# A two-layer decoder step on one core: pieces of the second output group placed one step earlier around the last two local groups

## The chip, the cores and the metric

The kernel runs on one core of a Trainium2 chip. The metric is device time in microseconds (us) of one execution. The kernel before was timed in three runs: 1675.39, 1678.78 and 1682.44 us, the median is 1678.78.

## What is computed

The reference is one inference step of a small hybrid decoder with two layers, D_MODEL 1024, over a prompt of 2048 tokens and a sample group of 8 x 8 tokens. Both layers have the same frame: an RMSNorm, one input projection, a token mixer and a cross-attention into 256 memory tokens, each multiplied by the SiLU of its gate, and one output projection that is added to the residual. The first layer's mixer pools over windows of rows. The second layer's mixer is local attention: 12 query heads on 4 shared key/value heads, blocks of 128 tokens that see their own and the previous block, with a learned sink in the softmax.

```python
z = rms_norm(x, norm_b[j]) @ w_in_b[j]
q, gq, qm, gm = jnp.split(z, [SWA_W, 2 * SWA_W, 2 * SWA_W + MEM_W], axis=-1)
q = rope_partial(rms_norm(q.reshape(B, T, N_Q_HEADS, HEAD_DIM), q_norm[j]), pos)
...
    o = swa_banded(q, k, v, sinks[j])
...
ys = o * jax.nn.silu(gq)
ym = memory_branch(qm, gm, mem_q_norm[li], mem_k[li], mem_v[li])
x = x + jnp.concatenate([ys, ym], axis=-1) @ w_out_b[j]
```

## The kernel before

All engines run a program written out by hand, and semaphores tie them together. The prompt is cut into 8 tiles of 256 tokens. The first layer goes over its 8 tiles and the sample group, then the second layer ("B") over the same 8 tiles and the sample group ("SB"). The loop of the second layer (`for it in range(TILES // 2): for p in range(2)`) has the same order of work for each tile on every engine.

Projections are exact to more than half precision: weights and activations are split into a high and a low f16 part, and three matmuls (high x high, high x low, low x high) stand for each product, accumulated in PSUM (`PARTS`). The gated activations that go into the output projection are eight chunks of 128 features, chunks 0 to 5 from the local attention and 6 and 7 from the memory branch. `split_out(part, t, g, kcs, halves, first, whole)` (matmul at line 791) issues the matmuls of output group g (256 features, two halves of 128) for the chunks in kcs, three for each chunk and half. So `split_out("B", t, 1, (0, 1), halves=(0,))` is six matmuls. With `first=True` and half 0 it first waits until the bank of PSUM is free:

```python
b = Z.wait_free(pe, part, t, f"out{g}") if first and 0 in halves else Z.bank(part, f"out{g}")
```

The banks of `ps_z` are a ring of two (class `Ring`): the names of a tile take them in turn, and a name waits until the reader of the name two places ahead has released it. The order of a tile of the second layer is

```python
"B": ["kv0", "kv1", "qa0", "qb0", "qa1", "qb1", "gm", "g0", "g1", "g2", *OUT],
```

with `OUT` being out0 to out3. g0 to g2 are the gates of the local attention; VectorE's `silu` (line 1714) reads them from `ps_z` and releases their banks.

Local attention works on six groups a tile, `W6 = [(0, 0), (1, 0), (0, 1), (1, 1), (0, 2), (1, 2)]` (block of 128 tokens, four heads). A group goes through these steps:

- `window_scores` on TensorE, then `window_front` on VectorE (masks and the maximum) and `window_exps` on ScalarE (line 1483)
- `window_back` on VectorE (the sum, its reciprocal, line 2158), then `window_norm` on GpSimd (line 2482)
- `window_transposes` on TensorE (line 1058, waits for `pw_norm`), then `window_weights` on VectorE (line 2166, two masked copies out of `ps_t`)
- `window_values` on TensorE (line 1070, waits until `ps_t` has been read), then `window_gated` on VectorE (line 2175, multiplies with the gate)

When both groups of a pair of chunks are gated, ScalarE takes the high half (`gate_highs`, line 1265), VectorE the low half as a subtraction (`gate_lows`, line 1740), and `glow_in` lets TensorE use these chunks. VectorE's order at the end of the tile is

```python
window_gated(t, 3)
window_weights(t, 4)
silu("B", t, "g2", 9, 4)
window_back(t, 5)
window_gated(t, 4)
gate_lows("B", t, 2, 2)
window_weights(t, 5)
window_gated(t, 5)
gate_lows("B", t, 3, 4)
```

In the same stretch ScalarE squares the next tile's input (`squares_x`, line 1222, after the high half of chunks 2 and 3), and GpSimd adds up the squares in three sums (`sums`, lines 2318, 2320, 2322). Their result is read by TensorE in `square_sums` (line 644) after the output groups 0 and 1 are whole. From there come the next tile's normalised input and its first projections.

Of the kernel before, what the change touches and what calls it, by code (L numbers as in the profile page):

```python
# [170 lines left out]
def build(nc, io):  # L171
    with ExitStack() as ctx:
# [461 lines left out]
        def _(pe):  # L634
# [150 lines left out]
            def split_out(part, t, g, kcs, halves=(0, 1), first=False, whole=False):  # L785

                b = Z.wait_free(pe, part, t, f"out{g}") if first and 0 in halves else Z.bank(part, f"out{g}")
                for half in halves:
                    for kc in kcs:
                        for ws, x in PARTS:  # L790
                            last = mm(ps_z[:, b, half * NT:(half + 1) * NT],  # L791
                                      w_out_split[:, g, ws, kc, half * P:(half + 1) * P], gate_parts[x][:, kc, 0:NT],
                                      start=(first and half == 0 and kc == kcs[0] and ws + x == 0),
                                      stop=(whole and half == 1 and kc == kcs[-1] and ws == 1))
                if whole:
                    last.then_inc(Z.full[b], 1)
# [257 lines left out]
            def window_transposes(t, i):  # L1054
                pe.wait_ge(pw_norm.sem, pw_norm.after("B", t, i))
                T.wait_free(pe, "B", t, f"ptw{i}")
                for e in range(4):
                    last = tr(ps_t[:, e * P:(e + 1) * P], sw[:, i % 2, e, :], ident)  # L1058
                last.then_inc(T.full[0], 1)

            def window_values(t, p, i):
                blk, gi = W6[i]
                T.wait_read(pe, "B", t, f"ptw{i}")
                V.wait_free(pe, "B", t, f"pvw{i}")
                own = 2 * p + blk
                for c in range(2):
                    for j, (s, w) in enumerate((((own - 1) % 4, ptp), (own, ptc))):
                        for par in range(2):
                            kv = 2 * ((2 * gi + c) // 3) + par
                            last = mm(ps_p[par * HD:(par + 1) * HD, c * P:(c + 1) * P],  # L1070
                                      v[:, s, kv * HD:(kv + 1) * HD], w[:, par * 2 + c, :],
                                      start=(j == 0), stop=(j == 1), skip_group_check=True)
                last.then_inc(V.full[0], 1)

            for it in range(TILES // 2):
                for p in range(2):
                    t = it * 2 + p
# [61 lines left out]
                    split_out("B", t, 0, (0, 1, 6, 7), halves=(0,), first=True)  # L1139
                    window_transposes(t, 4)  # L1140
                    split_out("B", t, 0, (0, 1, 6, 7), halves=(1,), first=True)
                    window_values(t, p, 4)
                    split_out("B", t, 1, (0, 1), halves=(0,), first=True)
                    window_transposes(t, 5)
                    split_out("B", t, 1, (6, 7), halves=(0,))
                    split_out("B", t, 1, (0, 1), halves=(1,), first=True)
                    window_values(t, p, 5)
                    split_out("B", t, 1, (6, 7), halves=(1,))
                    pe.wait_ge(glow_in.sem, glow_in.after("B", t, 2))
                    split_out("B", t, 0, (2, 3))  # L1150
                    split_out("B", t, 1, (2, 3))
# [1499 lines left out]
```

## Time and profile before

| | |
|---|---|
| median of three runs | 1678.78 us (1675.39 to 1682.44) |
| the profiled execution, its own time | 1681.61 us |
| its span, first to last instruction | 1679.5 us |
| TensorE matmul busy | 1560.9 us, 93% |
| VectorE busy | 956.4 us, 57% |
| ScalarE busy | 511.9 us, 30% |
| GpSimd busy | 506.6 us, 30% |
| mean granted clock of TensorE | 0.971 |
| HBM traffic | 71 GB/s over the span |

Busy shares are averages over stages of different kinds. Matmuls are pipelined and their ends are modelled, so the start of one to the start of the next is a better measure than the duration of one (0.27 us each, 0.11 us from start to start). In the order of time a row has the start in us from the beginning of the span, the duration, engine, line, operation, output <- inputs and count; an idle time of the engine ahead of it stands in brackets with what ended it. PE is TensorE, DVE is VectorE, ACT is ScalarE, POOL is GpSimd.

### The profile page before, as it was taken

To read this page: it belongs to the slowest core of one execution; us is meant where nothing else is said; L and a number is where in the kernel's file an instruction comes from. 1 tells how busy PE (TensorE), PEld (TensorE's weight loads), DVE (VectorE), ACT (ScalarE), POOL (GpSimd) and SP (SyncE) were. 2 spreads that over 40 slices of the span, in tenths; PEclk is the share of its full clock that TensorE was granted. 3 is DMA by queue.
4 is the path that set the end of the run, shared out by engine and by line. 5 is a ranking of instruction groups with operands and counts; after the bars stand their busy time and mean duration, and the time that the engine had idled before them with its cause. 6 is when DMAs were issued, how large, how long until landed. Compare 5 with 4: busy or idle time off the path is not lost.

```text
span 1679.5 us, 31237 instructions
## 1 busy us (share of the span) xinstructions
PE 1560.9 (93%) x13448; PEld 1223.0 (73%) x13448; DVE 956.4 (57%) x1846; ACT 511.9 (30%) x1227; POOL 506.6 (30%) x377
## 2 busy tenths in 40 slices
PE   4787999999999999978999999999999999999966
PEld 2466888888888888864775767768586685767745
DVE  6876465556646464624663836647375573846632
ACT  2442232232313232311432414224142331414320
POOL 3641425242425233221423313132131322224210
PEclk9999999999999999987999999999999999999985
DMA  9120213122121213178001010100101001010140
GB/s 399 48 82 29 98 60 117 66 86 101 51 101 51 102 62 114 55 279 348 1 7 45 2 51 2 39 13 2 51 2 51 1 2 51 2 51 2 41 148 26
DMA packets 27400, 119.12 MB, mean 71 GB/s; under 512 B 3488, under 2 KB 3936, under 8 KB 16480
## 3 DMA queue, kind: packets, MB, share of 16 engines
q1 hardware_dynamic: 25184, 108.33, 17.3%
q10 hardware_dynamic: 2080, 8.80, 1.3%
q8 instruction: 107, 1.75, 0.4%
q14 instruction: 29, 0.24, 0.0%
HBM read 81.38 MB, written 37.64 MB: 71 GB/s over the span
## 4 chain that ended last, share of the span: by engine, by line
PE 77%; DVE 13%; POOL 4%; ACT 2%; DMA 2%; issue 2%; SPq 0%; DVEq 0%; POOLq 0%; ACTq 0%
PE ps_z L677 23%; PE ps_z L791 18%; PE ps_z L666 16%; PE ps_z L781 3%; PE ps_s L1050 2%; PE ps_z L849 2%; PE ps_p L760 2%; DVE ph_sb L2166 2%; PE ps_t L750 2%; POOL tiny_sb L2313 2%; PE ps_p L1070 1%; PE ps_s L742 1%; POOL pm_sb L2337 1%; PE ps_t L1058 1%; DMA w_x_sb<-mem_vs 1%
## 5 line engine op out<-in xcount | busy, mean ns | idle before, releaser
L677 PE MATMUL ps_z<-xn_sb,w_in_sb 128*128 128x256 f16 (+1 forms) x4752 | 502.4, 264 | 5.1 <-DVE gate_sb L1714 4.2
L677 PEld LDWEIGHTS ps_z<-xn_sb,w_in_sb 128*128 128x128 f16 x4752 | 426.2, 98 | 62.4 <-issue 8.8
L791 PE MATMUL ps_z<-pm_sb,w_out_sb 128*128 128x256 f16 x2048 | 352.3, 274 | 3.3 <-DVE x_buf_sb L1780 3.3
L791 PE MATMUL ps_z<-gate_sb,w_out_sb 128*128 128x256 f16 x1024 | 280.3, 274 | 0.0
L2313 POOL TENSOR_TENSOR tiny_sb<-tiny_sb 128x2 f32<-128x2 f32 (+4 forms) x56 | 94.2, 1682 | 537.7 <-DVE tiny_sb L1681 305.5
L791 PEld LDWEIGHTS ps_z<-pm_sb,w_out_sb 128*128 128x128 f16 x2048 | 202.5, 99 | 32.2 <-issue 4.8
L666 PE MATMUL ps_z<-w_in_sb,xn_sb 128*128 128x512 f16 (+2 forms) x840 | 181.7, 376 | 0.0
L1672 DVE TENSOR_REDUCE tiny_sb<-scr_sb 128x8 f32<-128x512 f32 (+3 forms) x64 | 38.0, 593 | 237.3 <-ACT scr_sb L1230 157.4
L666 PEld LDWEIGHTS ps_z<-w_in_sb,xn_sb 128*128 128x128 f16 (+1 forms) x840 | 82.9, 99 | 94.1 <-issue 0.2
L1230 ACT ACTIVATE scr_sb<-ps_z,tiny_sb 128x256 f32<-128x256 f32 (+2 forms) x94 | 42.6, 489 | 347.1 <-PE ps_z L666 271.2
L2482 POOL TENSOR_TENSOR ph_sb<-ph_sb,tiny_sb 128x512 f32<-128x512 f32 x48 | 52.9, 1102 | 192.6 <-DVE tiny_sb L2158 192.6
L791 PEld LDWEIGHTS ps_z<-gate_sb,w_out_sb 128*128 128x128 f16 x1024 | 100.6, 98 | 11.6
L1483 ACT ACTIVATE ph_sb<-ph_sb,tiny_sb 128x128 f32<-128x128 f32 x192 | 74.5, 390 | 91.9 <-DVE tiny_sb L2148 91.9
L1780 DVE SCALAR_TENSOR_TENSOR x_buf_sb<-ps_z,tiny_sb,x_buf_sb 128x512 f32<-128x512 f32 x64 | 48.0, 750 | 91.5 <-PE ps_z L791 91.4
L2415 POOL TENSOR_TENSOR ph_sb<-ph_sb 128x1080 f32<-128x1080 f32 (+6 forms) x56 | 75.0, 1340 | 70.5 <-ACT ph_sb L1361 67.9
L666 PE MATMUL ps_z<-w_x_sb,xn_sb 128*128 128x512 f16 (+1 forms) x408 | 92.3, 387 | 3.4 <-issue 3.4
L2348 POOL TENSOR_TENSOR pm_sb<-pm_sb,tiny_sb 128x1024 f32<-128x1024 f32 x32 | 62.3, 1958 | 77.9 <-DVE tiny_sb L1707 77.9
L2318 POOL TENSOR_TENSOR big_sb<-big_sb 128x1024 f32<-128x1024 f32 x17 | 40.0, 2354 | 144.5 <-ACT big_sb L1222 144.5
L1244 ACT ACTIVATE xn_sb<-big_sb 128x2048 f16<-128x2048 f32 x18 | 34.4, 1910 | 149.5 <-DVE big_sb L1603 149.5
L666 PEld LDWEIGHTS ps_z<-w_x_sb,xn_sb 128*128 128x128 f16 (+1 forms) x408 | 40.8, 100 | 51.7 <-issue 7.3
L1275 ACT ACTIVATE scr_sb<-ps_z,tiny_sb 128x512 f32<-128x512 f32 (+1 forms) x72 | 46.7, 649 | 87.1 <-PE ps_z L677 85.4
L1280 ACT ACTIVATE big_sb<-ps_t 128x512 f32<-128x512 f32 (+1 forms) x68 | 39.5, 581 | 98.2 <-PE ps_t L750 82.0
(275 smaller groups left out, 2384.6 us busy)
## 6 DMA issues: line engine op xcount, KB each, us to landing
x_buf_sb<-x SPq DMA_DIRECT2D x18, 1024.0 KB, 4.8
w_x_sb<-w_b SPq DMA_DIRECT2D x14, 1024.0 KB, 4.8
x<-x_buf_sb SPq DMA_DIRECT2D x9, 1024.0 KB, 3.9
y<-x_buf_sb SPq DMA_DIRECT2D x9, 1024.0 KB, 3.9
w_in_sb<-w_in_a SPq DMA_DIRECT2D x8, 1024.0 KB, 25.5
w_in_sb<-parts ACTq DMA_DIRECT2D x8, 1024.0 KB, 13.2
parts<-ph_sb SPq DMA_DIRECT2D x14, 512.0 KB, 3.0
parts<-w_x_sb SPq DMA_DIRECT2D x14, 512.0 KB, 3.0
```

The costliest lines, as they stand in the source:

```text
L666: last = mm(out, xs[:, x, kc, tok:tok + n], w[:, gs[0]:gs[-1] + 1, ws, kc, :], start=(kc == 0 and ws + x == 0), stop=(kc == KC - 1 and ws ...
L677: last = mm(ps_z[:, b, half * NT:half * NT + n], w_split[:, g, ws, kc, half * P:(half + 1) * P], xs[:, x, kc, 0:n], start=(kc == 0 and ws ...
L781: last = mm(out, mix_w[:, blocks.index((o, i)), :], src, start=(i == ins[0]), stop=(i == ins[-1]))
L791: last = mm(ps_z[:, b, half * NT:(half + 1) * NT], w_out_split[:, g, ws, kc, half * P:(half + 1) * P], gate_parts[x][:, kc, 0:NT], start=( ...
L1230: last = f(scr[0:n, b, i * w:(i + 1) * w], ps_z[0:n, b, i * w:(i + 1) * w], ACT.Square, scale=unit if isinstance(unit, float) else unit[0:n])
L1275: f(pair[0], pair[1], ACT.Tanh, scale=halfunit).then_inc(scr_in.sem, 1)
L1483: f(sw[:, n % 2, e, :], sw[:, n % 2, e, :], ACT.Exp, bias=w_neg[:, n % 2, e:e + 1], scale=SCALE, accum_out=w_sum[:, n % 2, e:e + 1])
L1780: ve.scalar_tensor_tensor(x, ps_z[:, b].rearrange("p (c n) -> p c n", c=2)[:, :, 0:n], unit, x, ALU.mult, ALU.add).then_inc(Z.free[b], 1)
L2313: return tt(out, x, power[0:n, 0:w], ALU.pow)
L2348: tt(pm[:, blk], pm[:, blk], r, ALU.mult).then_inc(pm_norm.sem, 1)
L2415: own(tt(out[..., at:UW], src[..., at:UW], src[..., at // 2:UW - at // 2], ALU.add))
L2482: tt(sw[:, i], sw[:, i], r, ALU.mult).then_inc(pw_norm.sem, 1)
```

## The change

On TensorE alone, in the loop of the second layer, three pieces of output group 1 of six matmuls each stand one place earlier: chunks (0, 1) of half 0 ahead of the values of group 4, chunks (6, 7) of half 0 ahead of the transposes of group 5, chunks (6, 7) of half 1 ahead of the values of group 5. The order among the pieces of `split_out` stays as it was.

```diff
                     split_out("B", t, 0, (0, 1, 6, 7), halves=(0,), first=True)
                     window_transposes(t, 4)
                     split_out("B", t, 0, (0, 1, 6, 7), halves=(1,), first=True)
+                    split_out("B", t, 1, (0, 1), halves=(0,), first=True)
                     window_values(t, p, 4)
-                    split_out("B", t, 1, (0, 1), halves=(0,), first=True)
+                    split_out("B", t, 1, (6, 7), halves=(0,))
                     window_transposes(t, 5)
-                    split_out("B", t, 1, (6, 7), halves=(0,))
                     split_out("B", t, 1, (0, 1), halves=(1,), first=True)
+                    split_out("B", t, 1, (6, 7), halves=(1,))
                     window_values(t, p, 5)
-                    split_out("B", t, 1, (6, 7), halves=(1,))
                     pe.wait_ge(glow_in.sem, glow_in.after("B", t, 2))
                     split_out("B", t, 0, (2, 3))
                     split_out("B", t, 1, (2, 3))
```

## Rows read from the trace of the kernel before

**Rows 1.** The page: the chain that ended last, shares of the span by engine.
```profile
PE 77%; DVE 13%; POOL 4%; ACT 2%; DMA 2%; issue 2%; SPq 0%; DVEq 0%; POOLq 0%; ACTq 0%
```

**Rows 2.** TensorE's waits, whole span: us in total, times, longest us.
```profile
PE ps_p L1070 <- DVE ph_sb L2166: 12.0, 16, 1.3
```

**Rows 3.** The last chain in order of time: start us, us, what.
```profile
862.30 6.00 PE ps_z L791 x54
...
1576.52 6.00 PE ps_z L791 x54
```

**Rows 4.** Order of time, TensorE, 953 to 971 us (one tile's output stretch).
```profile
957.63 0.27 PE L791 MATMUL ps_z<-pm_sb,w_out_sb 128*128 128x256 f16 x1
959.19 1.09 PE L1070 MATMUL ps_p<-ph_sb 128*64 128x128 f32 x16 [1.29 <-DVE ph_sb L2166]
...
961.19 0.66 PE L1058 MATMUL ps_t<-small_sb,ph_sb 128*128 128x128 f32 x4
...
963.23 1.09 PE L1070 MATMUL ps_p<-ph_sb 128*64 128x128 f32 x16
964.26 0.28 PE L791 MATMUL ps_z<-pm_sb,w_out_sb 128*128 128x256 f16 x1
...
970.16 0.50 PE L644 MATMUL ps_p<-ones_sb,big_sb 128*128 128x1 f32 x4
```

**Rows 5.** Order of time, VectorE, the same stretch.
```profile
957.86 1.28 DVE L2166 TENSOR_TENSOR ph_sb<-ps_t,small_sb 128x512 f32<-128x512 f32 x2
959.05 0.68 DVE L1714 SCALAR_TENSOR_TENSOR gate_sb<-scr_sb,ps_z 128x512 f32<-128x512 f32 x1
...
960.33 0.48 DVE L2175 SCALAR_TENSOR_TENSOR gate_sb<-ps_p,tiny_sb,gate_sb 128x256 f32<-128x256 f32 x1 [0.32 <-PE ps_p L1070]
960.74 0.95 DVE L1740 TENSOR_TENSOR gate_sb<-gate_sb,pm_sb 128x512 f16<-128x512 f32 x1
961.89 1.29 DVE L2166 TENSOR_TENSOR ph_sb<-ps_t,small_sb 128x512 f32<-128x512 f32 x2 [0.20 <-PE ps_t L1058]
...
965.55 1.23 DVE L1740 TENSOR_TENSOR gate_sb<-gate_sb,pm_sb 128x512 f16<-128x512 f32 x1 [0.70 <-ACT pm_sb L1265]
```

**Rows 6.** Order of time, GpSimd, the same stretch.
```profile
960.10 1.04 POOL L2482 TENSOR_TENSOR ph_sb<-ph_sb,tiny_sb 128x512 f32<-128x512 f32 x1 [4.76 <-DVE tiny_sb L2158]
961.73 2.36 POOL L2318 TENSOR_TENSOR big_sb<-big_sb 128x1024 f32<-128x1024 f32 x1 [0.59 <-ACT big_sb L1222]
964.17 1.27 POOL L2320 TENSOR_TENSOR big_sb<-big_sb 128x512 f32<-128x512 f32 x1
965.52 0.73 POOL L2322 TENSOR_TENSOR big_sb<-big_sb 128x256 f32<-128x256 f32 x1
```

**Rows 7.** Order of time, ScalarE, the same stretch.
```profile
959.76 1.90 ACT L1222 ACTIVATE big_sb<-x_buf_sb 128x2048 f32<-128x2048 f32 x1
964.89 0.63 ACT L1265 ACTIVATE pm_sb<-gate_sb 128x512 f16<-128x512 f32 x1 [3.24 <-DVE gate_sb L2175]
```

**Rows 8.** Instructions of two VectorE lines: duration ns min/median/max, first and last start us.
```profile
L1740 DVE TENSOR_TENSOR gate_sb<-gate_sb,pm_sb x64: 658/692/1246, 144.5 to 1577.7; 128x512 f16<-128x512 f32 x64
...
L2156 DVE TENSOR_TENSOR tiny_sb<-tiny_sb x48: 150/159/860, 823.0 to 1571.8; 128x4 f32<-128x4 f32 x48
```

**Rows 9.** Order of time, GpSimd and VectorE, about 937 and 152 us.
```profile
935.82 1.89 POOL L2348 TENSOR_TENSOR pm_sb<-pm_sb,tiny_sb 128x1024 f32<-128x1024 f32 x1 [2.73 <-DVE tiny_sb L1707]
936.87 0.86 DVE L2156 TENSOR_TENSOR tiny_sb<-tiny_sb 128x4 f32<-128x4 f32 x1 [0.62 <-ACT tiny_sb L1485]
...
150.54 2.35 POOL L2318 TENSOR_TENSOR big_sb<-big_sb 128x1024 f32<-128x1024 f32 x1 [25.69 <-ACT big_sb L1222]
151.62 1.35 DVE L1623 TENSOR_SCALAR lo_sb<-small_sb,tiny_sb 128x128 f32<-128x128 f32 x1
152.96 1.27 POOL L2320 TENSOR_TENSOR big_sb<-big_sb 128x512 f32<-128x512 f32 x1
```

**Rows 10.** One stretch: us, engines' busy us (x instructions), PEclk, DMA share, GB/s.
```profile
953.60:970.20 16.60, 15.06 (x154) 12.68 (x154) 11.32 (x23) 5.23 (x13) 6.79 (x5) 1.00 0.00 1
```

## The prediction

> **What bounds the kernel now.** I read the page first [rows 1]: the chain that ended last is 77% TensorE, so a change in the order of its work counts only through the gaps that it closes or opens. The list of waits says where such gaps are [rows 2]: the values of the local groups (line 1070) waited for VectorE's masked weights (line 2166) 16 times, 12.0 us in all, which is two waits in each of the eight tiles of the second layer. The eight tiles repeat each other: the chain in order of time has an entry for line 791 in each, 54 matmuls in 6.00 us, the first at 862.30 and the last at 1576.52, seven periods of 102.03 [rows 3]. The remaining views are orders of time in the second tile, where this entry comes at 964.3.
>
> In it I follow TensorE [rows 4]. The last piece of group 0, half 1, starts at 957.63, and matmuls of this kind follow each other at 0.109 us (964.26 to 970.16 for 54), so TensorE is free at 957.74. The values of group 4 start only at 959.19. That is gap 1, 1.45 us. The six matmuls of out1 (0,1) follow, then the transposes of group 5 at 961.19, 0.31 us after the last of the six could have ended (gap 2), and the values of group 5 at 963.23, 0.24 us after the twelve matmuls between (gap 3). So 2.0 us a tile, 16 us in the kernel, is the most that any order here could win.
>
> **Who ends each gap.** VectorE's rows [rows 5]: the masked weights of group 4 run from 957.86 to 959.14, and the values start 0.05 later. Gap 2 ends with GpSimd's normalisation of group 5 (960.10 for 1.04) [rows 6], gap 3 with the masked weights of group 5, 961.89 to 963.18. The reader should also see what stands between them on VectorE: the SiLU of g2 (line 1714, 959.05 for 0.68), the gating of group 4 (line 2175, 960.33), the low half of gate chunks 2 and 3 (line 1740, 960.74), and only then the weights of group 5.
>
> **The change, step by step.** No instruction is added or taken away, none is a DMA, and no other engine's order is edited. Three groups of six matmuls move.
>
> Step 1, out1 (0,1) half 0 goes ahead of the values of group 4. It carries first=True for half 0, so it waits for its bank of ps_z to come free. The order of the Z ring has g2 at place 9 and out1 at place 11 of the tile, and two banks: the same one. g2 is released by the SiLU at line 1714, and on VectorE that stands behind the masked weights of group 4, for which the values wait. So the piece that was to fill gap 1 can't start before 959.73 + 0.05 = 959.78 [rows 5], later than the values started before. The six matmuls take 0.65, and the values of group 4, queued behind them, start at 960.43 instead of 959.19: **1.24 us later**. Gap 1 grows from 1.45 to 2.04.
>
> Step 2, out1 (6,7) half 0 goes ahead of the transposes of group 5. The values of a group issue for 1.03 (963.23 to 964.26), those of group 4 now to 961.46; six matmuls bring it to 962.12; by then the normalisation of group 5 has been done since 961.14, so gap 2 is gone. The transposes start at 962.12 against 961.19, and VectorE could read them 0.70 later, as before (961.19 to 961.89), at 962.82.
>
> Step 3, out1 (6,7) half 1 goes ahead of the values of group 5. TensorE has twelve matmuls after the transposes (1.31 after about 0.45) and reaches the values at about 963.9. It then depends on when VectorE has the weights of group 5.
>
> Step 4 is what the delay of step 1 does on VectorE. The gating of group 4 waits for the values: their last matmul ends 1.09 after their start, at 961.52, and the gating starts 0.05 later, 961.57; the low half of chunks 2 and 3 follows 0.41 later as in the rows, at **961.98** instead of 960.74. GpSimd starts its first sum of squares, 128x1024, at **961.73** and holds on to 964.09 [rows 6]. That start does not move: it follows ScalarE's squares, 959.76 for 1.90 [rows 7], which wait for nothing that is changed. Now the low half is a subtraction of two SBUF tensors, and such operations stand still while GpSimd runs one of its own on SBUF tensors [rows 8, 9]: line 1740 takes 0.658 at best, and in this tile 0.95 and 1.23, where it met a GpSimd instruction; both ended 0.55 and 0.53 after that instruction's end (961.14 to 961.69, 966.25 to 966.78). A four-element addition (line 2156) that takes 0.159 in the median took 0.86, from 936.87 to 937.73, against a GpSimd instruction that ended at 937.71. And the very instruction at issue, line 2318, did it at 150.54 to 152.89: a scaling of one 128x128 SBUF tensor (line 1623) started at 151.62 and ended at 152.97, just after the release. So the low half will hold VectorE until 964.09 + 0.54 = 964.63. In order behind it, the masked weights of group 5 start at about 964.57 and end at 965.86 (1.29), and the values of group 5 start at **965.91** instead of 963.23. Gap 3 grows from 0.24 to 2.0.
>
> On this the Trainium skill speaks against the change too ("SBUF — State Buffer", where it treats the shared port pair): VectorE operations with two SBUF inputs and GpSimd operations that read SBUF take one lock, whoever starts first keeps it for the whole instruction, and the other blocks fully. The rows agree as to the blocking; by the letter of the rule the whole 0.66 of the subtraction would come after the release, 0.12 a tile more than the 0.54 that the rows show, and the sum would be 17 us instead of 16.
>
> **The sum.** The values of group 5 issue for 1.03, to 966.94. Six of the 54 matmuls that followed them now lie ahead, so 48 remain, 5.25 us, and the sums of the square (line 644), the next step, start at 972.19 instead of 970.16: **+2.03 us a tile, +16.2 for eight**. Two covers must hold. The chain to gate chunk 4 (gating 0.48, ScalarE's high half 0.63 [rows 7], low half) runs from the values' last result at 967.00 to about 968.9; TensorE wants it after 24 of the 48 matmuls, at 969.56, so it stays hidden by 0.6. GpSimd's remaining sums are put back by the subtraction by about half a microsecond, to 966.8, and are wanted at 972. All that follows in the tile is released by what has moved with it, so I take nothing off later.
>
> The profiled execution took 1681.61 us; with the sum 1697.8. It lies 2.8 above the median of the runs shown, 1678.78, which with the sum gives **1695.0**.
>
> **Rivals.**
> A. As above, 1695.0. The uncertain term is the stand-still of the low half. From below it is nothing (its 0.66 then lies ahead of the transposes' result); from above it loses the port a second time (D). I take the stand-still for all of line 2318, because the rows show just that instruction doing it [rows 9].
>
> B, on the other side: not slower. The low half gets the port first, or is not held. It decides at one point, whether 961.98 lies before or after GpSimd's 961.73, a margin of 0.25 that I worked out and did not see. Then the weights of group 5 follow the transposes, 962.82 to 964.11, the values start at 964.16, and the tile is 0.28 longer: +2.2 us, **1681**. For it: the margin is only a quarter of a microsecond. Against it: the end of the SiLU's row would have to be 0.25 early as a release, while the release that ended gap 1 came 0.05 after its row's end; and the port went to GpSimd on a lead of only 0.03 at 965.52 against 965.55.
>
> C. The bank does not bind, and the change does what its order suggests. Then the six matmuls run in gap 1, the values of both groups start when they did, and six matmuls fewer follow them: 0.65 a tile, 5.2 in all, **1673.6**, 0.3% faster. Against it stand the order of the ring and the place of the SiLU.
>
> D. VectorE loses the port again, to the second sum of GpSimd (964.17 to 965.44). The low half then ends at 965.98, and the tile is 3.4 longer: **1706**. Against it: at 152.89 the waiting VectorE operation got through before the second sum, at 152.96, had run [rows 9].
>
> E. TensorE's clock. With two gaps of 2.0 us inside eight microseconds it could fall. In the stretch of 953.6 to 970.2, with gap 1 at 1.45, the granted clock is 1.00, that is 2.4 GHz throughout [rows 10]. At 1.2 GHz the 48 matmuls would take another 5.25, for eight tiles 42 us, **1737**. The Trainium skill ("TensorE: Matmul & The Clock Gate", Part 1) has an idle array fall back to 1.2 GHz; no row here shows that at gaps of 2 us.
>
> **How the numbers follow.** Chances: A 0.81, B 0.10, C 0.04, D 0.03, E 0.02. About 0.5%, 8.4 us, is what a measurement of this kernel can tell from no change. A, D and E lie beyond it on the slow side: 0.85, after taking a little off for the size of A. B and C lie within it: 0.13. Faster by more would need over half of all three gaps, and no case gives that: 0.02. A's own range is 1690 to 1700: 3 or 4 us of scatter between runs, as those shown have (1675.39 to 1682.44), and a microsecond for the rule above. A alone is just 8 in 10, and scatter takes some of it, so the range goes down to B: 1680 to 1700.
>
> **What would show it.** Right: the first piece of out1 waits for line 1714 (gap of about 2.0); the values of group 4 start 1.2 us later in the tile; line 1740 has one instance in each tile of about 2.6 us that ends half a microsecond after line 2318; the values of group 5 wait about 2.0 for line 2166; the period is 104.05. Wrong: a line 1740 of 0.7 with line 2318 starting after it is B; a first piece at 957.74 is C; a line 1740 of 4 us is D; a granted clock below 1 in the tile is E.

## The result, and the profile after

The changed kernel takes 1695.8 us (median of four runs, 1694.7 to 1697.12), the kernel before beside it 1679.74 (1675.39 to 1682.44). The ratio is 1.0094, with a 95% interval of 1.0078 to 1.0110: slower, by 16 us. The profiled execution took 1697.12 us, its span is 1695.1.

The waits of TensorE over the whole span (us in total, times, longest) hold a new one at the top, and the old one of [rows 2] has not gone:

```profile
PE ps_z L791 <- DVE gate_sb L1714: 15.1, 8, 1.9
PE ps_p L1070 <- DVE ph_sb L2166: 13.9, 15, 1.7
```

The first is step 1 of the prediction: in each of the eight tiles the first matmul of out1 waits for the SiLU of g2, which releases its bank. The second counts other waits than it did. Before, its 16 were those of the values of group 3 (0.22 each) and of group 4 (gap 1, 1.29 each) in the eight tiles. Now the eight of group 3 remain, and the other seven are gap 3, about 1.74 each; the second tile has none, since its matmuls ahead of gap 3 were slow (see the section on the prediction). Gap 1 no longer shows as a wait for the masked weights, since they are done 1.4 us before TensorE gets there.

The chain in order of time gives the period. It shows the 48 matmuls that are left behind the values of group 5, where [rows 3] had 54:

```profile
864.67 5.35 PE ps_z L791 x48
...
1592.89 5.35 PE ps_z L791 x48
```

Seven periods lie between the two, so one is 104.03 us, against 102.03 before: 2.00 us a tile, 16.0 in eight. The whole change of time lies in this stretch of the tile.

To lay a tile of after over the one of before, I take the values of group 3 as its zero; the work that leads to them is not touched. Before, in the tile that the prediction follows, they start here:

```profile
953.63 1.09 PE L1070 MATMUL ps_p<-ph_sb 128*64 128x128 f32 x16 [0.22 <-DVE ph_sb L2166]
```

I take the third tile of after, because the second has a stretch at a lower clock. There TensorE does this (order of time, values, transposes and the first matmul of out1):

```profile
1059.35 1.09 PE L1070 MATMUL ps_p<-ph_sb 128*64 128x128 f32 x16 [0.21 <-DVE ph_sb L2166]
...
1065.51 0.28 PE L791 MATMUL ps_z<-pm_sb,w_out_sb 128*128 128x256 f16 x1 [1.89 <-DVE gate_sb L1714]
...
1066.27 1.09 PE L1070 MATMUL ps_p<-ph_sb 128*64 128x128 f32 x16
...
1067.96 0.60 PE L1058 MATMUL ps_t<-small_sb,ph_sb 128*128 128x128 f32 x4
...
1071.61 1.09 PE L1070 MATMUL ps_p<-ph_sb 128*64 128x128 f32 x16 [1.74 <-DVE ph_sb L2166]
...
1077.89 0.51 PE L644 MATMUL ps_p<-ones_sb,big_sb 128*128 128x1 f32 x4
```

VectorE and GpSimd in the same tile:

```profile
1064.78 0.68 DVE L1714 SCALAR_TENSOR_TENSOR gate_sb<-scr_sb,ps_z 128x512 f32<-128x512 f32 x1
...
1067.41 0.48 DVE L2175 SCALAR_TENSOR_TENSOR gate_sb<-ps_p,tiny_sb,gate_sb 128x256 f32<-128x256 f32 x1 [1.67 <-PE ps_p L1070]
1067.82 2.54 DVE L1740 TENSOR_TENSOR gate_sb<-gate_sb,pm_sb 128x512 f16<-128x512 f32 x1
1070.28 1.27 DVE L2166 TENSOR_TENSOR ph_sb<-ps_t,small_sb 128x512 f32<-128x512 f32 x2
```
```profile
1067.45 2.36 POOL L2318 TENSOR_TENSOR big_sb<-big_sb 128x1024 f32<-128x1024 f32 x1 [0.59 <-ACT big_sb L1222]
1069.89 1.60 POOL L2320 TENSOR_TENSOR big_sb<-big_sb 128x512 f32<-128x512 f32 x1
```

The reader sees the whole mechanism in these lines. The SiLU ends at 1065.46, and the first matmul of out1 starts 0.05 later. The values of group 4 follow, late; with them the gating (line 2175) is late, and the low half (line 1740) starts at 1067.82, 0.37 behind GpSimd's first sum. It takes 2.54 us for a subtraction that takes 0.66 alone, and ends at 1070.36, 0.55 after the sum's end. Seven tiles are like this one. In the second the low half starts later, 0.60 behind the sum, and takes 2.30; its end is again 0.56 after the sum's end. Behind it the masked weights (line 2166) are late, and TensorE waits 1.74 us for them. Even the second sum bears the trace of it: 1.60 against 1.27 in [rows 6], and it starts 0.47 before the low half ends.

### The profile page after: what moved, and what is told of

It reads as the page before. It is cut to its first block, busy times and chain, and to the rows that moved or that the text cites. A ratio compares the mean times of both kernels' runs of the same rounds, so it can differ in the third digit from the quotient of the medians.

```text
span 1695.1 us, 31237 instructions
## 1 busy us (share of the span) xinstructions
PE 1560.6 (92%) x13448; PEld 1223.7 (72%) x13448; DVE 963.8 (57%) x1846; ACT 511.9 (30%) x1227; POOL 509.1 (30%) x377
## 4 chain that ended last, share of the span: by engine, by line
PE 77%; DVE 14%; POOL 3%; ACT 2%; DMA 2%; issue 2%; SPq 0%; DVEq 0%; POOLq 0%; ACTq 0%
PE ps_z L677 23%; PE ps_z L791 18%; PE ps_z L666 16%; PE ps_z L781 3%; PE ps_s L1050 2%; PE ps_z L849 2%; PE ps_p L1070 2%; PE ps_p L760 2%; PE ps_t L750 2%; DVE ph_sb L2166 2%; POOL tiny_sb L2313 2%; DVE gate_sb L1740 1%; PE ps_s L742 1%; POOL pm_sb L2337 1%; DMA w_x_sb<-mem_vs 1%
## 5 line engine op out<-in xcount | busy, mean ns | idle before, releaser
L1265 ACT ACTIVATE pm_sb<-gate_sb 128x512 f16<-128x512 f32 x64 | 40.1, 626 | 114.2 <-DVE gate_sb L2175 47.2
```

## The experiments

Times in the tile are given from the start of the values of group 3. They are alike in all tiles of each trace, to 0.02, but for tiles with a lower clock: the six under the mark *, and the first tile of the kernel whose sums wait (told at the end of the section on the prediction). The columns are the start of the values of group 4, of the values of group 5, and of the sums of the square (line 644), where the next step begins. The table was worked out from the order of time of each trace. The ratios are estimated from all executions and can differ in the fourth place from the quotient of the medians.

```
kernel                          group 4   group 5   line 644   ratio to before (95%)
before                            5.56      9.60     16.53     1
after                             6.92     12.25     18.53     1.0094 (1.0078 to 1.0110)
sums wait for the low half        6.91     10.59     16.87     1.0012 (1.0004 to 1.0021)
wait for the bank alone           6.15      9.83     16.76     1.0012 (1.0003 to 1.0021)
first move alone                  6.91     12.25     20.8 *    1.0184 (1.0170 to 1.0198)
second and third move alone       5.56      9.89     16.17     0.9976 (0.9966 to 0.9985)
SiLU first                        6.16      9.83     16.11     0.9984 (0.9975 to 0.9993)
gap filled                        6.37      9.60     15.87     0.9966 (0.9953 to 0.9979)
* 20.6 to 20.8 in six tiles, 19.18 in two
```

**The sums wait for the low half.** The changed kernel with one wait more, on GpSimd:

```diff
+                    pool.wait_ge(glow_in.sem, glow_in.after("B", t, 2))
                     sums("B", t, 0)
```

> The changed kernel, and GpSimd's sums of squares (lines 2318 to 2322) wait for the low half of gate chunks 2 and 3, so that these two can't meet; the wait of out1 for its bank stays. Theory: of the 2.0 us a tile, most is the low half standing still (2.54 in the changed kernel against 0.66). Without it the values of group 4 still start 6.92 after those of group 3 (5.56 before), the masked weights of group 5 follow the transposes, and the values of group 5 start at about 10.65 after those of group 3 instead of 12.25 (9.60 before); the tile is about 0.4 longer than before: 1680 + 3 = 1683 us. Rival: the wait for the bank (or TensorE's clock behind the longer gaps) is the loss by itself; then the time stays near 1696.

Measured: 1684.41 us against 1681.79 for the kernel before on that chip. Taking away the meeting of the two instructions gives back 1.66 of the 2.00 us a tile (18.53 to 16.87). The added wait also starts the sums 1.1 us later in the tile; line 644 still does not wait for them. In the second tile of this kernel, VectorE's low half and GpSimd's sum, which starts behind it:

```profile
963.74 0.68 DVE L1740 TENSOR_TENSOR gate_sb<-gate_sb,pm_sb 128x512 f16<-128x512 f32 x1
```
```profile
964.50 2.36 POOL L2318 TENSOR_TENSOR big_sb<-big_sb 128x1024 f32<-128x1024 f32 x1 [1.72 <-DVE gate_sb L1740]
```

The rival, that the wait for the bank is the loss by itself, has fallen: the wait is still there (15.0 us in all, eight times), and the tile is 0.34 longer than before, with what the other two moves win already in it.

**The wait for the bank alone.** The kernel before, with the wait put ahead of the values of group 4 and the matmuls left behind them:

```diff
+                    Z.wait_free(pe, "B", t, "out1")
                     window_values(t, p, 4)
                     split_out("B", t, 1, (0, 1), halves=(0,), first=True)
```

> The kernel before, with only the wait for out1's bank put ahead of the values of group 4; the matmuls stay where they were. The values of group 4 are late by about 0.6 instead of 1.36, and the low half of chunks 2 and 3 starts about 0.4 ahead of GpSimd's first sum, so it takes the port first. Theory (the loss has a threshold, the point at which the low half comes behind the sum's start): low half of 0.7 in every tile, tile longer by 0.34 or so, 1680 + 2.7 = 1682 to 1683 us. Rival (the loss grows in proportion to the delay of the values of group 4, 2.0 for 1.36): 0.87 a tile, 1687 us.

Measured: 1683.49 us, ratio 1.0012, 0.23 us a tile. The values of group 4 are 0.59 late, and the low half starts ahead of the sum. In the second tile VectorE's subtraction takes its ordinary time, and it is GpSimd that waits a little (2.51 for its first sum, 2.36 otherwise); one line more in this kernel, so line numbers are higher by one:

```profile
960.96 0.68 DVE L1741 TENSOR_TENSOR gate_sb<-gate_sb,pm_sb 128x512 f16<-128x512 f32 x1
```
```profile
961.37 2.51 POOL L2319 TENSOR_TENSOR big_sb<-big_sb 128x1024 f32<-128x1024 f32 x1 [0.60 <-ACT big_sb L1223]
```

A delay of 0.59 costs 0.23 and one of 1.36 costs 2.00; in proportion the first would have cost 0.87. So the loss has a step between the two. In the kernel before, the low half starts 0.99 ahead of the sum (960.74 against 961.73), so a delay of about 1.0 puts it behind; that the step lies just there is argued, since no run has a delay between 0.59 and 1.36.

**The first move alone.**

```diff
+                    split_out("B", t, 1, (0, 1), halves=(0,), first=True)
                     window_values(t, p, 4)
-                    split_out("B", t, 1, (0, 1), halves=(0,), first=True)
                     window_transposes(t, 5)
                     split_out("B", t, 1, (6, 7), halves=(0,))
```

> Only the first of the three moves: out1 (0,1) half 0 ahead of the values of group 4. Theory: this move holds the whole loss, and the other two take back a little of it. The low half stands still as in the changed kernel, the values of group 5 start 12.25 after those of group 3, and 54 instead of 48 matmuls follow: 2.65 a tile longer than before, 1680 + 21 = 1701 us. Rival: the loss comes from the moves around the transposes and the values of group 5; then 1680 to 1683.

Measured: 1712.81 us, 12 more than expected. Up to the values of group 5 each tile is as expected (6.91, 12.25), and in two of the eight tiles the rest is too (19.18). In the other six line 644 comes at 20.6 to 20.8. In all eight tiles the wait for the masked weights is longer than in the changed kernel (2.35 against 1.74), because fewer matmuls stand ahead of it; in these six TensorE's granted clock falls behind it. The stretches of the second and third tile from the start of gap 1 to the values of group 5, and from these on (us, busy us of PE, PEld, DVE, ACT, POOL, then PEclk, DMA share, GB/s):

```profile
961.52:969.62 8.10, 3.92 (x40) 2.92 (x38) 6.39 (x10) 3.92 (x11) 4.99 (x3) 0.99 0.00 0
969.62:977.42 7.80, 7.75 (x64) 6.59 (x65) 1.59 (x3) 0.63 (x1) 0.73 (x1) 0.79 0.01 2
```
```profile
1067.71:1075.81 8.10, 3.92 (x40) 2.92 (x38) 6.38 (x10) 3.92 (x11) 4.99 (x3) 1.00 0.00 0
1075.81:1083.61 7.80, 7.75 (x79) 6.94 (x80) 2.08 (x4) 0.63 (x1) 0.77 (x2) 1.00 0.01 2
```

The same stretch of the same order has 64 matmuls of the trace in one tile and 79 in the other. In the first of them the granted clock from 969.67 to 972.42 is 0.50, and the values of group 5 take nearly twice as long (1.97 against 1.09):

```profile
963.57 0.28 PE L791 MATMUL ps_z<-pm_sb,w_out_sb 128*128 128x256 f16 x1 [1.88 <-DVE gate_sb L1714]
...
969.67 1.97 PE L1070 MATMUL ps_p<-ph_sb 128*64 128x128 f32 x16 [2.35 <-DVE ph_sb L2166]
```

So the clock costs 1.4 to 1.6 us in each of six tiles, 9.4 in all. The kernel before was 1.8 slower on that chip than the 1680 of the expectation; both together are 11.2 of the 11.8 us above 1701. The theory holds as far as its own terms go (this move has the whole loss, 2.65 a tile where the clock stayed), and rival E of the prediction was at work beside it.

**The second and third move alone.**

```diff
                     split_out("B", t, 1, (0, 1), halves=(0,), first=True)
+                    split_out("B", t, 1, (6, 7), halves=(0,))
                     window_transposes(t, 5)
-                    split_out("B", t, 1, (6, 7), halves=(0,))
                     split_out("B", t, 1, (0, 1), halves=(1,), first=True)
+                    split_out("B", t, 1, (6, 7), halves=(1,))
                     window_values(t, p, 5)
-                    split_out("B", t, 1, (6, 7), halves=(1,))
```

> Only the second and third move: out1 (6,7) half 0 ahead of the transposes of group 5 and (6,7) half 1 ahead of its values; out1 (0,1) half 0 stays behind the values of group 4. Theory: nothing waits for the bank, the low half starts 7.11 after the values of group 3 as before, ahead of the sum; the values of group 5 start at about 9.98 (9.60 before) and 48 matmuls follow: 0.27 a tile shorter, 1680 - 2 = 1677 to 1678 us, a little faster than before. Rival: these two moves cost by the later transposes, 0.3 to 0.5 a tile: 1682 to 1684.

Measured: 1677.14 us against 1681.79, ratio 0.9976: these two moves win 0.36 us a tile, 2.9 in eight, which lies within the interval of the ratio; the rest of the 4.65 between the medians is not in this stretch. They close gap 2 and put the six matmuls into the time that VectorE takes for the masked weights. What the change lost, it lost by its first move.

**The SiLU first.** The changed kernel, with two lines of VectorE's order exchanged, so that the bank comes free before the masked weights of group 4 are done:

```diff
+                    silu("B", t, "g2", 9, 4)
                     window_weights(t, 4)
-                    silu("B", t, "g2", 9, 4)
```

> The changed kernel with VectorE's SiLU of g2 ahead of the masked weights of group 4, so that out1's bank comes free before those weights are there. Theory: the wait for the bank is where the delay starts, so without it the low half of chunks 2 and 3 starts at 7.7 after the values of group 3, 0.4 ahead of GpSimd's first sum, and takes the port. Values of group 4 at 6.16 (5.56 before, 6.92 changed: the SiLU takes 0.6 of its own), of group 5 at about 10.0, 48 matmuls behind them, next step at 16.26 (16.53 before): 0.27 a tile shorter than before, 1681.8 - 2 = 1679 to 1680 us. Rival: the moved matmuls themselves, or a clock that falls behind TensorE's gaps, cost the time: 1690 or more.

Measured: 1678.99 us against 1681.41, ratio 0.9984. All three moves stand, and the kernel is faster than before by 0.42 us in the tile (16.11, where 16.26 was expected). The loss starts from the order of the SiLU against the bank, then, and not from the moves as such: with the bank released earlier TensorE waits for it 0.7 instead of 1.9, and the low half takes 0.68, ahead of the sum. In the second tile:

```profile
961.76 0.68 DVE L1740 TENSOR_TENSOR gate_sb<-gate_sb,pm_sb 128x512 f16<-128x512 f32 x1
```
```profile
962.16 2.50 POOL L2318 TENSOR_TENSOR big_sb<-big_sb 128x1024 f32<-128x1024 f32 x1 [0.59 <-ACT big_sb L1222]
```

**The gap filled.** On TensorE twelve matmuls of out1 stand ahead of the values of group 4, the transposes of group 5 right behind these values, and the other twelve ahead of the values of group 5; on VectorE the SiLU comes first and the low half after the masked weights of group 5; GpSimd's sums wait for the low half. Against the kernel before:

```diff
+                    split_out("B", t, 1, (0, 1), halves=(0,), first=True)
+                    split_out("B", t, 1, (6, 7), halves=(0,))
                     window_values(t, p, 4)
-                    split_out("B", t, 1, (0, 1), halves=(0,), first=True)
                     window_transposes(t, 5)
-                    split_out("B", t, 1, (6, 7), halves=(0,))
                     split_out("B", t, 1, (0, 1), halves=(1,), first=True)
+                    split_out("B", t, 1, (6, 7), halves=(1,))
                     window_values(t, p, 5)
-                    split_out("B", t, 1, (6, 7), halves=(1,))
...
+                    silu("B", t, "g2", 9, 4)
                     window_weights(t, 4)
-                    silu("B", t, "g2", 9, 4)
                     window_back(t, 5)
                     window_gated(t, 4)
-                    gate_lows("B", t, 2, 2)
                     window_weights(t, 5)
+                    gate_lows("B", t, 2, 2)
...
+                    pool.wait_ge(glow_in.sem, glow_in.after("B", t, 2))
                     sums("B", t, 0)
```

> A version built on what the runs showed. SiLU of g2 first; twelve matmuls of out1, half 0, ahead of the values of group 4; the transposes of group 5 right behind these values; the other twelve ahead of the values of group 5; VectorE takes the masked weights of group 5 ahead of the low half of chunks 2 and 3, and GpSimd's sums wait for that low half. Theory: values of group 4 at 6.4 after those of group 3, of group 5 at 9.60 as before, and 48 matmuls behind them instead of 54: next step at 15.9 (16.53 before, 16.17 with the second and third move alone), 0.65 a tile, 1681.8 - 5 = 1676 to 1677 us. Rival: GpSimd's later sums meet the low half of chunks 4 and 5 and TensorE waits for it: 16.5 or more, 1681 or more.

Measured: 1675.24 us against 1681.41, ratio 0.9966. It has the lowest median of the kernels run, though its interval overlaps with that of the second and third move alone, and the shortest tile, as expected: 9.60 and 15.87. Several things are changed at once here, and what each of them is worth was not run. Its second tile, TensorE's order of time:

```profile
956.85 0.28 PE L791 MATMUL ps_z<-pm_sb,w_out_sb 128*128 128x256 f16 x1 [0.69 <-DVE gate_sb L1714]
...
958.26 1.09 PE L1070 MATMUL ps_p<-ph_sb 128*64 128x128 f32 x16
959.45 0.66 PE L1058 MATMUL ps_t<-small_sb,ph_sb 128*128 128x128 f32 x4
...
961.48 1.09 PE L1070 MATMUL ps_p<-ph_sb 128*64 128x128 f32 x16
```

The wait for the bank is down to 0.69, and nothing else here is a wait that the profile lists. The low half of chunks 4 and 5 does meet the first sum (1.22 us instead of 0.66), but it is done before TensorE wants it, and the rival, 16.5 or more, did not come:

```profile
963.80 1.22 DVE L1740 TENSOR_TENSOR gate_sb<-gate_sb,pm_sb 128x512 f16<-128x512 f32 x1 [0.70 <-ACT pm_sb L1265]
```
```profile
962.11 2.37 POOL L2318 TENSOR_TENSOR big_sb<-big_sb 128x1024 f32<-128x1024 f32 x1 [2.71 <-DVE gate_sb L1740]
```

This low half starts 1.69 behind the sum and ends 0.54 after it. With 0.37 and 0.60 in the changed kernel, that is three different starts and nearly the same end: the sum's end sets it, not the start.

## Why the prediction was right

The forecast was 1695.0 in a range of 1680 to 1700, slower with a chance of 0.85; measured were 1695.8, and A is what happened.

Step 1 held as it was put: out1 shares its bank with g2, and the piece starts 0.05 after the SiLU's end. Only a size was off: the six matmuls and the change to the values take 0.76 (1065.51 to 1066.27) and not 0.65, so the values of group 4 are 1.36 late and not 1.24.

Step 2 and step 3 held, and by themselves win, as the run of these two moves alone shows.

Step 4 decided the matter and held: the low half starts behind the sum (by 0.37, forecast 0.25), stands still for the rest of it, and ends 0.55 after it (forecast 0.54). Since that end is set by GpSimd, the 0.12 that step 1 had missed changed nothing later: the values of group 5 start at 12.25, and 12.28 was forecast (965.91 less 953.63). The sum was 2.03 a tile and 2.00 was measured. That neither this 0.12 nor the slow matmuls of the second tile (below) show in the total is luck: the stand-still covered both. On the shared port pair the Trainium skill ("SBUF — State Buffer", section "SBUF: two separate sides") says that whoever starts first keeps it for the whole instruction. The traces agree, in both directions: VectorE takes 2.54 instead of 0.66 as the second in the changed kernel, GpSimd 2.51 instead of 2.36 as the second with the bank's wait alone. By its letter the low half would end 0.66 after the sum; it ends 0.55 after. What the runs show is that the second of the two stands still until the first is done; that a shared port is the reason is the word of the Trainium skill, which no run here tests.

Of the two covers, that of gate chunk 4 held: its low half ran from 1073.94 to 1074.63, and TensorE wanted it after 24 of the 48 matmuls, 2.6 us behind the end of the values' 1.03 (1072.64), at 1075.26. GpSimd's remaining sums held too: the last of them is done 5.6 us before line 644.

B was the closest rival. The run whose sums wait is the change without the stand-still, and so shows B's price: 0.34 a tile, for a forecast of 0.28. The run with the bank's wait alone shows B's condition, the low half 0.4 ahead of the sum and not held. C could not come, for the bank. D did not come: the second sum waited (1.60).

E was given 0.02 and was half right, which the total does not show. In the second tile of the changed kernel the granted clock did fall, behind gap 1 (three stretches: gap 1, from the values of group 4 on, and the rest):

```profile
959.40:962.20 2.80, 0.92 (x8) 0.51 (x6) 2.29 (x6) 2.80 (x11) 0.39 (x1) 1.00 0.00 0
962.20:966.40 4.20, 4.20 (x32) 3.25 (x31) 2.76 (x3) 1.16 (x1) 3.53 (x3) 0.59 0.02 4
966.40:973.80 7.40, 7.29 (x74) 6.23 (x73) 3.06 (x5) 0.63 (x1) 1.80 (x2) 1.00 0.00 0
```

That tile is no longer than the others (18.52), since the slow matmuls ran in the time in which TensorE would have waited for the low half anyway. With the sums held back there is one such tile too, the first, with 0.68 in the stretch behind gap 1, and there it costs what it takes: group 5 at 12.21 instead of 10.59, 1.6 us.

```profile
858.20:863.50 5.30, 5.23 (x39) 4.17 (x38) 2.37 (x4) 1.14 (x1) 2.86 (x2) 0.68 0.01 3
```

## What to carry to other kernels

Before work is moved into an engine's gap, ask what that work itself waits for, and whether this comes from behind the very thing for which the engine waits; here a PSUM bank was freed by the instruction that stood behind the masked weights. Then follow the delay to the engines that it reaches and compare the new starts with what GpSimd does at that time: whether VectorE's subtraction started 0.4 us ahead of GpSimd's sum or 0.4 us behind it made a loss of 0.2 or of 2 us a tile. A stretch with two causes of delay shows only the longer one, so take away the visible one in a run before calling the other free.

## What was not expected

TensorE's granted clock fell to half its level, from 2.4 to 1.2 GHz, behind waits of 1.9 to 2.4 us, in some tiles and not in others of the same order: in one of eight in the changed kernel and with the sums held back, in six of eight with the first move alone, where waits of 1.88 and 2.35 us follow each other. It cost 1.4 to 1.6 us a tile where nothing covered it. The Trainium skill ("TensorE: Matmul & The Clock Gate", Part 1) has an idle array fall back to 1.2 GHz, and the tiles that fell agree: 0.50 of full speed from 969.67 to 972.42 with the first move alone. Why one tile falls and the next, with the same waits, does not is open: no run here separates it.
